# Two transformer blocks with 64 experts on one core: the fallback for full experts behind the final norm, combinations split between the turns, and products without use at the routing

## The reference, cut to what matters

```python
def reference(x, mem, ...):                  # x: 1 x 256 x 1024, float32
    x = first_block(x, mem, ...)             # two layers of attention and gated linear attention
    return second_block(x, ...)

def second_block(...):
    ...                                      # HGRN2 mixer, latent attention, gates
    x = x + y @ w_out[l]
    h = rmsnorm(x, ffn_norm_w[l])
    x = x + hierarchical_moe(h, ...)         # top-1 of 8 groups, top-2 of its 8 experts
    return rmsnorm(x, final_norm_w)

# each of 64 experts, for the rows routed to it:
    hid = silu(xb @ w1[e]) * (xb @ w3[e])    # 1024 -> 512, twice
    return (hid @ w2[e]) * wts[:, None]      # 512 -> 1024
```

## Time and profile before

| | |
|---|---|
| time, median of 3 runs | 1675.73 us (1672.19 to 1676.8) |
| profiled execution, its own time | 1675.66 us |
| its span | 1673.4 us |
| TensorE busy | 1501.7 us (90%) |
| VectorE busy | 637.7 us (38%) |
| ScalarE busy | 510.5 us (31%) |
| mean granted clock of TensorE | 0.944 |
| transfers of the expert weights | 2 MB each, 30.6 us from issue to landing (median) |

### The profile page before, as it was taken

One profiled execution on the slowest core, in us unless ns is written; L12 is line 12 of the kernel. 1 busy time (PEld: TensorE's weight loads), 2 busy tenths in 40 slices (PEclk: granted clock), 3 DMA queues, 4 the chain that ended last, 5 costly groups with the idle time before them and its releaser, 6 DMA issues.

```text
span 1673.4 us, 20485 instructions
## 1 busy us (share of the span) xinstructions
PE 1501.7 (90%) x8585; PEld 893.1 (53%) x8585; DVE 637.7 (38%) x1416; ACT 510.5 (31%) x1089; POOL 0.2 (0%) x4
## 2 busy tenths in 40 slices
PE   7998999898999999979999998898888888988886
PEld 5785878577787788743444343333333333333332
DVE  6666567465755566741121221211211212212112
ACT  5666466556554565400111111101010011010111
POOL 0000000000000000000000000000000000000000
PEclk9999899899999999978999999999999999999988
DMA  7242243233423346689999999999999999999994
GB/s 271 101 151 101 101 139 121 81 130 116 152 61 115 134 153 249 234 351 392 428 427 427 428 427 428 427 427 428 427 428 427 428 428 426 427 427 428 427 427 166
DMA packets 74450, 496.40 MB, mean 297 GB/s; under 512 B 6224, under 2 KB 10608, under 8 KB 49392
## 3 DMA queue, kind: packets, MB, share of 16 engines
q1 hardware_dynamic: 74352, 495.03, 72.8%
HBM read 493.96 MB, written 1.05 MB: 296 GB/s over the span
## 4 chain that ended last, share of the span: by engine, by line
PE 60%; DMA 26%; DVE 8%; ACT 5%; issue 1%; SPq 0%; DVEq 0%; ACTq 0%
DMA arena<-in_expert_w 26%; PE ps L1094 20%; PE ps L1437 8%; PE ps L1444 7%; PE ps L1458 5%; PE ps L1467 4%; DVE arena L1981 3%; PE ps L1091 2%; ACT arena L1569 2%; PE ps L1421 2%; PE ps L1074 1%; PE ps L1190 1%; ACT arena L1572 1%; DVE w_lo L1981 1%; PE ps L1125 1%
## 5 line engine op out<-in xcount | busy, mean ns | idle before, releaser
L1978 DVE COPY arena<-ps 128x512 f32<-128x512 f32 (+2 forms) x203 | 119.5, 589 | 596.9 <-PE ps L1437 466.4
L1437 PE MATMUL ps<-arena 128*32 128x512 f32 x2048 | 254.4, 616 | 50.6 <-DMA arena<-in_expert_w 46.1
L1572 ACT ACTIVATE arena<-ps 128x512 f32<-128x512 f32 (+6 forms) x244 | 121.6, 500 | 465.8 <-PE ps L1437 208.9
L1981 DVE TENSOR_TENSOR w_lo<-arena,w_hi 128x512 fp32r<-128x512 f32 (+2 forms) x304 | 199.8, 672 | 133.0 <-ACT w_hi L1572 131.4
L1444 PE MATMUL ps<-arena 128*128 128x512 f32 x512 | 238.7, 609 | 0.0
L1572 ACT ACTIVATE w_hi<-arena 128x512 fp32r<-128x512 f32 (+2 forms) x320 | 193.0, 620 | 101.3 <-PE ps L1094 88.3
L1569 ACT ACTIVATE arena<-ps 128x128 f32<-128x128 f32 (+2 forms) x140 | 48.9, 373 | 453.4 <-PE ps L1467 425.6
L1437 PEld LDWEIGHTS ps<-arena 128*32 128x32 f32 x2048 | 57.0, 111 | 242.4 <-issue 131.6
L1094 PE MATMUL ps<-w_hi,hT_hi 128*128 128x512 f32 (+3 forms) x448 | 177.8, 397 | 5.9 <-DVE w_lo L1981 3.6
L1444 PEld LDWEIGHTS ps<-arena 128*128 128x128 f32 x512 | 93.0, 192 | 150.6 <-issue 148.9
L1094 PE MATMUL ps<-w_hi,hT_lo 128*128 128x512 f32 (+3 forms) x448 | 169.5, 378 | 0.0
(11 more groups left out here) (153 smaller groups left out, 1438.0 us busy)
## 6 DMA issues: line engine op xcount, KB each, us to landing
arena<-in_expert_w SPq DMA_DIRECT2D x191, 2048.0 KB, 30.6
arena<-in_w_in SPq DMA_DIRECT2D x23, 2048.0 KB, 7.8
arena<-in_w_out SPq DMA_DIRECT2D x6, 2048.0 KB, 8.0
arena<-in_w_in SPq DMA_DIRECT2D x3, 1536.0 KB, 6.4
arena<-in_w_mem_kv SPq DMA_DIRECT2D x2, 2048.0 KB, 9.1
arena<-in_w_branch_hgrn SPq DMA_DIRECT2D x2, 2048.0 KB, 7.8
arena<-in_w_branch_mla SPq DMA_DIRECT2D x2, 2048.0 KB, 7.8
arena<-in_mla_w_uq SPq DMA_DIRECT2D x2, 1152.0 KB, 5.6
```

What stands on the lines that cost most here:

```text
L1437: o = e.matmul(B[32 * j:32 * j + 32, :], Xs[:, k, q:q + 32], Wn[:, k, :], start=i == 0, stop=i == 1)
L1572: return e.activation(o, i, ACTF.Copy, scale=scale)
L1978: return e.tensor_copy(o, i)
L1981: return e.tensor_tensor(o, a, b, op)
```

## The change

- The planner's list gets two steps `warm` of two products each, behind the last half of `y @ w_out` and ahead of the second part of the logits; seven such products stand ahead of the ranks, and two ahead of `scales(0)`. Each is the identity by 512 float32 columns, into a bank of its own (`P.idle`), which nobody reads.
- `combine(ex - 1, 1)` moves behind `turn_h(ex, 0)`; `combine(ex - 1, 0)` stays between the two `up`. The marks "h turned" and "combined" are given for each half. ScalarE's silu starts when the first half is turned, and `turn_h(ex, 1)` waits for it.
- `turn_c(ex)` moves behind `down(ex, 1)` in groups 0 to 6; in group 7 it stands ahead of `down`. VectorE's copy of it moves behind its copy of the result.
- The last expert is in the loop again, in the same order as the others. The fallback stands at each engine's end: on TensorE behind `combine(63, 1)`, on ScalarE and VectorE behind the output's last pieces, on SyncE behind the issue of the four output transfers and ahead of the last wait for them. Its code adds its sums to the residual and makes the final norm and the output again.

```diff
         add("residual", 2, 1, bs)
-        A, B = get(), get()
+        A, B, P.idle = get(), get(), get()
+        add("warm", 2)
         add("turn x", 4, A, B)
         add("parts", 1, 0)
         add("mean x")
         add("take x", 4, B)
+        add("warm", 2)
         add("logits", 4, P.logits)
...
+            def warm(n):
+
+                w.wait_ge(s_wr, 32)
+                room(plan.idle)
+                for _ in range(n):
+                    e.matmul(ps(plan.idle)[:, :], ident, mem(184, 512), start=True, stop=True)
...
+            warm(7)
             w.wait_ge(*at("sel"))
...
-                    w.wait_ge(*ever("ct", 8 * (g - 1) + k))
+                    w.wait_ge(*ever("ct", 8 * (g - 1) + k - 1))
...
-                    elif t and h:
-                        i.then_inc(mark(pe_moe, ("combined", ex)), 1)
+                    elif t:
+                        i.then_inc(mark(pe_moe, ("combined", ex, h)), 1)
...
             def turn_h(ex, h):
                 w.wait_ge(*at("h", ex, h))
-                if ex:
+                if h:
+                    w.wait_ge(*at("sil", ex))
+                elif ex:
                     w.wait_ge(*at("hid", ex - 1))
...
+            warm(2)
             scales(0)
             for n, k in enumerate(FIRST):
                 gather(0, n, k)
-            for ex in range(NE - 1):
+            for ex in range(NE):
                 g = ex // 8
                 up(ex, 0)
                 if ex:
                     combine(ex - 1, 0)
-                    combine(ex - 1, 1)
                 up(ex, 1)
...
                 turn_h(ex, 0)
-                turn_h(ex, 1).then_inc(mark(pe_moe, ("h turned", ex)), 1)
-                turn_c(ex)
+                if ex:
+                    combine(ex - 1, 1)
+                turn_h(ex, 1)
                 if g < 7:
                     if ex % 8 == 0:
                         scales(g + 1)
                     gather(g + 1, 0, ex % 8)
+                else:
+                    turn_c(ex)
                 down(ex, 0)
                 down(ex, 1)
-            combine(NE - 2, 0)
-            combine(NE - 2, 1)
-            book.also("end", "moe", "pe")
+                if g < 7:
+                    turn_c(ex)
+            combine(NE - 1, 0)
+            combine(NE - 1, 1)
 
             w.wait_ge(*at("flag"))
             over = e.value_load(flagi[0:1, 0:1])
             with e.If(over > 0):
...
             e.end_ifs()
-
-            w.met.clear()
-            up(NE - 1, 0)
-            turn_h(NE - 1, 0).then_inc(mark(pe_moe, ("h turned", NE - 1)), 1)
-            turn_c(NE - 1)
-            up(NE - 1, 1)
-            w.wait_ge(*at("sil", NE - 1))
-            turn_h(NE - 1, 1).then_inc(mark(pe_moe, ("last turned",)), 1)
-            down(NE - 1, 0)
-            down(NE - 1, 1)
-            combine(NE - 1, 0)
-            combine(NE - 1, 1)
...
         def sync(e):
...
             for t in range(2):
                 for h in range(2):
                     cs = slice(h * 512, h * 512 + 512)
                     w.wait_ge(*at("out", t, h))
                     e.dma_start(out[0, t * 128:t * 128 + 128, cs], done_[:, t, cs]).then_inc(s_out, 16)
+            w.wait_ge(*at("flag"))
+            over = e.value_load(flagi[0:1, 0:1])
+            with e.If(over > 0):
+                w.wait_ge(s_out, 64)
...
+            e.end_ifs()
+            w.met.clear()
             w.wait_ge(s_out, 64)
```

More of the change, by code:

```diff
@@ L1512, in tensor @@
             with e.If(over > 0):
-                w.wait_ge(*at("end", "moe", "act"))
-                w.wait_ge(*at("end", "moe", "dve"))
+                w.wait_ge(*at("out", 1, 0))
+                w.wait_ge(*at("out", 1, 1))
                 for n in range(2 * NE):
                     ex, t = divmod(n, 2)
-                    for i, B in ((2, B4), (3, B5)):
+                    for i, B in ((0, B4), (1, B5)):
                         w.wait_ge(f_w[0], 16 * (ex + 1))
@@ L1921, in scalar @@
             run(es, es, ACTF.Exp).then_inc(mark(act_moe, ("es exp",)), 1)
-            def silu(ex):
-                w.wait_ge(*at("h turned", ex))
+            for ex in range(NE):
+                w.wait_ge(*at("up", ex, 0))
+                w.wait_ge(*ever("h turned", ex - 1, 0))
+                copy(H1s.rearrange("p (j f) -> p j f", j=4), B4[:, :].rearrange("p (f j) -> p j f", j=4)).then_inc(
+                    mark(act_moe, ("h", ex, 0)), 1)
+                w.wait_ge(*at("h turned", ex, 0))
@@ L1939, in scalar @@
-            for ex in range(NE - 1):
-                first_h(ex)
-                silu(ex)
-                down(ex, 0)
-            book.also("end", "moe", "act")
-            w.wait_ge(*at("flag"))
-            over = e.value_load(flagi[0:1, 0:1])
-            with e.If(over > 0):
-                w.wait_ge(*at("end", "moe", "pe"))
-                w.wait_ge(*at("end", "moe", "dve"))
-                for n in range(2 * NE):
-                    w.wait_ge(fp_up, n + 1)
-                    if n:
-                        w.wait_ge(fp_turn, n)
-                        w.wait_ge(fv_hid, n)
-                    e.activation(H1s, B4[:, :], ACTF.Silu, scale=SS[3][:, n % 2:n % 2 + 1]).then_inc(fa_silu, 1)
-                w.wait_ge(fv_sum, 4 * NE)
@@ L1957, in scalar @@
-            e.end_ifs()
-            w.met.clear()
-            first_h(NE - 1)
-            silu(NE - 1)
-            use(EXP_LN)
-            down(NE - 1, 0)
-            down(NE - 1, 1)
+                if ex == NE - 1:
+                    use(EXP_LN)
+                for h in range(1 + (ex == NE - 1)):
+                    w.wait_ge(*at("y", ex, h))
+                    w.wait_ge(*ever("combined", ex - 1, h))
+                    copy(Ys[:, 512 * h:512 * h + 512], (B4, B5)[h][:, :]).then_inc(mark(act_moe, ("ys", ex, h)), 1)
@@ L2644, in vector @@
-            e.end_ifs()
-            w.met.clear()
-            turned_c(NE - 1)
-            second_h(NE - 1)
-            w.wait_ge(*at("last turned"))
-            hidden(NE - 1)
+                    w.wait_ge(*at("y", m, 1))
+                    w.wait_ge(*ever("combined", m - 1, 1))
+                    copy(Ys[:, 512:1024], B5[:, :]).then_inc(mark(dve_moe, ("ys", m, 1)), 1)
+                w.wait_ge(*at("in ct", m))
+                w.wait_ge(*ever("combined", m - 2, 1))
+                copy(CT[m % 2], B7[:, 0:256]).then_inc(mark(dve_moe, ("ct", m)), 1)
@@ L2652, in weigh @@
+                if g < 7 and m % 8 == 7:
+                    weighted(g + 1)
+                if g == 7 and m < NE - 1:
+                    w.wait_ge(*at("y", m, 1))
+                    w.wait_ge(*ever("combined", m - 1, 1))
+                    copy(Ys[:, 512:1024], B5[:, :]).then_inc(mark(dve_moe, ("ys", m, 1)), 1)
             def weigh(t):
@@ L2754, in sync @@
                     e.dma_start(out[0, t * 128:t * 128 + 128, cs], done_[:, t, cs]).then_inc(s_out, 16)
+            w.wait_ge(*at("flag"))
+            over = e.value_load(flagi[0:1, 0:1])
+            with e.If(over > 0):
+                w.wait_ge(s_out, 64)
+                for ex in range(NE):
+                    if ex:
+                        w.wait_ge(fp_down, 2 * ex)
+                    for i, (name, k) in enumerate((("expert_w1_2", 8), ("expert_w3_2", 8), ("expert_w2_2", 4))):
+                        e.dma_start(slots[i].rearrange("p (k n) -> p k n", k=k),
+                                    A[name][0, ex].rearrange("(p k) n -> p k n", k=k)).then_inc(f_w[i], 16)
+                for t in range(2):
+                    w.wait_ge(fv_out, t + 1)
+                    e.dma_start(out[0, t * 128:t * 128 + 128, :], done_[:, t, :]).then_inc(f_out, 16)
+                w.wait_ge(f_out, 32)
+            e.end_ifs()
+            w.met.clear()
             w.wait_ge(s_out, 64)
```

159 lines of the change are left out of this document (78 added, 81 removed).

## The result

After: median 1666.89 us of 13 runs (1663.09 to 1670.23); before, on the same chip, 1674.1 us of 13 (1670.14 to 1676.8). The ratio is 0.9959 with a 95% interval from 0.9948 to 0.997: faster by 0.4%. The forecast was 1668.0 in a range of 1663 to 1673.5. The profiled execution took 1664.84 us.

The account below looks back on a forecast made before the run. Transfers bind 52% of the span, so only the start, the way from the last loads and the end can change. 1675.66 - 2.7 (transfers) - 5.35 (last down) - 1.6 (its clock) + 1.7 (branch) = 1667.7, about 1668; range 1663 to 1673.5.

Parts of the forecast that it names:

- The last expert: Expert 63: down starts at 1648.35 instead of 1656.41, 8.05 us earlier, 2.7 of it by transfers and 5.35 new.
- Down's clock: Last expert's down runs at the full clock, about 1.95 us instead of 3.53, another 1.6 us gained.
- The branch at the end: Passing the fallback at the engines' ends costs 4.15 - 2.5 = 1.7 us, the pause less what the landing covers.
- Rival D: At the end, SyncE's passing of the branch takes 8.3 us, twice TensorE's: +4.15, 1672 us; chance 0.09.
- The transfers: Weight loads end 2.2 to 3.2 us earlier because gaps ahead of them close; 2.7 us taken.
- The delay up to expert 0: Products at the routing make ranks, scales and expert 0's second half turn late, the turn by 2.3 us (730.85).
- the gap ahead of load 12: In expert 1, the DMA gap of 2.8 us until load 12 is issued shrinks to 0 to 1.05 us.
- Rival A: The clock holds through expert 0's pause, winning 3.9 us there; load 9 at 737, 1664 us; chance 0.13.
- Rival B: The clock falls in TensorE's waits for the last loads, so the last expert stays slow: +5, 1673 us; chance 0.12.
- Rival C: In expert 0 the 1.6 + 0.3 us are not saved, or products drain longer: +2 to +4, 1671 us; chance 0.10.
- the 1.6 + 0.3 us of the order in expert 0: Expert 0: earlier silu saves 1.6 us of waiting, and moving VectorE's copy of turn_c saves 0.3 us.
- Rival E: Products at the routing, 710 to 727, don't hold the clock: +13.3, 1681 us, slower; chance 0.06.

Follow-up runs that it names:

- e5: The changed kernel with the fallback and its branches taken out of all four engines; ratio 0.995 to before.
- e7: The changed kernel with combine(62, 1), for the last expert alone, back between its two ups; ratio 0.9956 to before.
- e2: The kernel before with the thirteen products alone, old order, fallback at its old place; ratio 0.9998 to before.
- e3: The changed kernel without the thirteen products; ratio 0.995 to before.
- e9: The changed kernel with five products instead of thirteen, plus three in TensorE's 3.1 us wait in expert 0 and one in expert 1; 1658.22 us, ratio 0.9909 to before.
- e10: e9 and e7 together: five products, filled pauses, and combine(62, 1) between the last expert's two ups; ratio 0.9902 to before.
- e14: e10 with three more products of 256 columns in TensorE's wait for load 189 ahead of the last expert; ratio 0.9905 to before.
- e1: The kernel before with the fallback at the engines' ends and the last expert in the loop, old order, no products; 1668.12 us, ratio 0.9955 to before.
- e12: The changed kernel with fourteen products instead of seven ahead of the ranks; ratio 0.998 to before.

## Why the prediction was right, point by point

**The last expert** carries the gain, as forecast. From R, down came 7.35 us earlier; forecast were 8.05 (2.7 by the transfers, 5.35 by the way to it). It is 1649.06 on the scale of before, against 1648.35. The 0.7 that is missing is in this trace load 190, which released up 1 at 1643.1 on that scale instead of 1642.35. Down's clock gave 1.6 us, as forecast (3.53 to 1.92). From down's end to the output's issue lie 8.92 us, before 8.97.

**The branch at the end** was mis-sized: +1.0 us measured, +1.7 forecast. The term was the pause on TensorE less the landing of the output, 4.15 - 2.5. No run bears that subtraction out: the span ends 0.4 us behind the last landing in after as before, where 1 to 2 were forecast, and the 1.0 lies in the output's issues and landings, which come later (e5). Rival D (+4.15 more) is out. The sum from R is then -7.35 - 1.61 - 0.05 + 0.97 = -8.04, and the spans show 961.32 - 969.36 = -8.04; forecast were -7.95. Errors of 0.7 on both sides cancel in it; that the sum is right to 0.1 us is luck.

**The transfers** were forecast at -2.7. In the trace of after the gaps give 1.06 (load 9) + 0.5 + 0.85 = 2.4, and load 190 is there 1.9 earlier (1643.1 against 1645.0). The way there was another in its parts. The delay up to expert 0 came as worked out: ranks at 716.15 on the scale of before (716.25), scales at 718.3 (718.3), the second half's turn at 730.85 (730.85). But load 9 was issued at 739.5 and not at 740.9, since the clock fell only behind that turn, and down took 3.01 instead of 3.64. The step that failed in this trace is the gap ahead of load 12: 2.0 us, not 0 to 1.05. Load 12 itself came at 756.45, within the forecast 755.1 to 756.7. But the gap begins when the loads ahead of it are through, and these had started 1.0 earlier with load 9: before, with load 9 at 740.52, load 12 was 2.8 us too late at 757.89, so its limit was 755.1; now it was 754.0, and 756.45 is 2.4 late. What was won at load 9 was mostly lost again at load 12. The sum of both stayed near the forecast.

This is the execution and not the code. e7 has the code of after up to the last expert, and e5 has it but for the branch. In their traces the clock was low in expert 0 and full in expert 1, and they go the way of the forecast. The second half's turn of e7, and its stretch from 756 to 760, which lies about where the gap of 2.0 us is in after:

```profile
732.44 1.92 PE L1482 MATMUL ps<-arena 128*128 128x32 f32 x8 [3.11 <-DVE arena L1980]
...
756.00:760.00 4.00, 4.00 (x26) 1.26 (x22) 1.02 (x2) 0.60 (x1) 0.00 (x0) 1.00 1.01 430
```

Load 9 is issued 36.32 (e5) and 36.73 (e7) from R, forecast was 36.86 (740.9 less 704.04), and load 12 at 50.71 and 50.46 without a gap ahead of it. Load 189 lets up 0 of the last expert start 933.02 and 933.12 from R, 1.1 to 1.2 earlier than in after (934.21). So the transfers gained some 3.0 us in these two traces and 1.9 in that of after, and the forecast 2.7 lies between.

**Rival A** happened by a third in the trace of after (0.83 us in the turn and 0.63 in down, of its 3.9), but the products aren't what did it. With them, the turn and down took 1.92 and 3.49 us in e7 and 1.92 and 3.64 in e2; without them, 1.25 and 2.83 in e3. e9 shows the rival in full, with products where the pause is; e10 and e14 show it in part. **Rival B** did not happen in the trace of after, but e7's trace has it: the clock fell in the same 2 us wait. It cost 1.7 us there (2.75 + 4.53 against 1.92 + 3.70), not 5, because the clock was back at up 1 and stayed so in down. **Rival C** is out: the 1.6 + 0.3 us of the order in expert 0 were saved. From the start of the second half's turn to down's lie 8.29 us before, 5.53 in after and 5.71 in e3, without products; less what the clock gave in the turn (0.83 and 0.66), both are 1.9 shorter. **Rival E** is out: the clock stood at 1.00 up to the pause.

**What the sum hid.** It had no price for each part alone. The runs give them: the branch's move 0.45% (e1), the products nothing or a loss (e2 0.9998; e3 against after), the order some 0.1% at most (e3 against e1, intervals overlapping; by the places 1.7 us from R, with what the clock gave e3 in down of expert 0: 2.83 us against 3.57). The whole is no more than its first part, since thirteen products of 0.86 us stand in 5.4 us of idle time and end before the pause ahead of the second half's turn, behind which the clock is lost.

What stays open: why the clock falls in a wait of 2 us for a load in some executions (e7, e10) and not in others (after, e9), why it falls at the turn in one execution and at down in another of the same code (e7, after), and what makes R differ by 6 us between executions of the same code.

## What to carry to other kernels

A block that is never run still costs time where it stands in an engine's stream, since the engine has to pass it: put it where its engine has nothing more to do, and look for idle time of the bounding engine that "waited for nothing". Products without use are worth something only inside a wait, up to a little less than its length, and above all inside the last wait ahead of the work that the next transfer hangs on: five plus four of them there gave 0.4% against none (e9 against e3), and thirteen, seven of them in a wait that holds four, gave nothing or cost 1.4 us. One profiled execution can mislead: what looked like a third of rival A in after is gone in e7, with the same code. When two profiled executions are compared, count from a point that both reach with the same code.

## What was not expected of the hardware

- The same branch costs TensorE 4.15 us (4.42 in e2) ahead of the last expert, beside transfers at 226 GB/s, and 1.0 us at the kernel's end. Whether the other transfers make the difference, or that all four engines pass it at different times, wasn't tried.
- The last transfers of weights don't run at 427 GB/s. From 1638 on they move about half, with a DMA share of about half, in after:

```profile
1638.00:1640.00 2.00, 1.62 (x4) 0.38 (x2) 0.00 (x0) 0.37 (x1) 0.00 (x0) 1.00 0.53 216
1640.00:1642.00 2.00, 1.32 (x14) 0.42 (x16) 0.00 (x0) 0.00 (x0) 0.00 (x0) 1.00 0.52 203
```

  From 1642 to 1644 it is 178 GB/s. Nothing was tried on this.
- Behind the same wait of 3.1 us in expert 0, the same turn took from 1.08 us (full clock) to 1.92 (low clock), and it doesn't go with what stood ahead. With the thirteen products, so that TensorE had no pause for 24 us (30 in e12), it is 1.08 in after, 1.36 in e5, 1.70 in e12, 1.92 in e2 and e7. With the pauses at the routing left as they were, it is 1.91 before, 1.22 in e1 and 1.25 in e3 and e6. So the 24 us without a pause, the argument for rival A, don't hold the clock there.
